# Two transformer blocks on one core: masks by TensorE, table spread by SyncE, token halves at a layer's beginning, rests of weights by GpSimd

## What is computed

```python
h = x @ w_in        # 1024 -> 4 branches' q, k, v, four gates, a merge vector
y_mla = causal softmax attention(low-rank q, k, v with rms norm and rope)
y_sb  = stick-breaking attention: A[t,s] = sigmoid(z[t,s]) * prod_{s<j<t} (1 - sigmoid(z[t,j])), s < t
y_fox = causal softmax attention with log_decay = cumsum(log_sigmoid(f))
y_mem = softmax attention over 256 memory rows
merged = sum_n sigmoid(merge_r @ w_merge_up)_n * ((y_n * silu(gate_n)) @ w_branch[n])
x = layer_norm(alpha * x + merged @ w_out)
```

```python
z = rms_norm(x) @ w_in_2
o_a = softmax attention (rms-normed q, k, axial rope)
o_b = softmax attention in a window of 128 with a sink
o_c = neighbourhood attention with a table of relative position biases (rpb_c)
o_d = (softmax(q1 k1) - lam * softmax(q2 k2)) v, then rms norm
x = x + concat(o_n * silu(g_n)) @ w_out_2       # and a final rms norm at the end
```

## Time and profile before

| | us |
|---|---|
| runs | 1534.04, 1537.66, 1539.85 |
| the profiled execution | 1534.89 |
| its span, first to last instruction | 1533.1 |
| TensorE busy | 1413.1 (92%) |
| VectorE busy | 869.9 (57%) |
| ScalarE busy | 709.6 (46%) |
| GpSimd busy | 366.7 (24%) |
| mean granted TensorE clock | 0.975 of full speed |

### The profile page before, as it was taken

How to read it: one execution, slowest core, us unless ns; L and a number is a source line. 1 busy time by engine, 2 the same in 40 slices (tenths; PEclk the granted TensorE clock), 3 DMA queues, 4 the chain that set the end, 5 groups by cost and what they waited for, 6 DMA issues and landing times.

```text
span 1533.1 us, 21207 instructions
## 1 busy us (share of the span) xinstructions
PE 1413.1 (92%) x8026; PEld 1091.0 (71%) x8026; DVE 869.9 (57%) x1657; ACT 709.6 (46%) x1525; POOL 366.7 (24%) x265
## 2 busy tenths in 40 slices
PE   7999899999989999999997899988998899988997
PEld 6767576777977677777786766665776766665776
DVE  4555337467662553465577565457656465557655
ACT  3555345455234554455543454445444344445443
POOL 2232131245231322223541112320111112320111
PEclk9999999999999999999998899998999899998999
DMA  6413620225242221112263232511313332411311
GB/s 227 111 30 87 158 83 15 78 67 213 97 151 56 52 88 56 55 45 62 91 214 98 60 77 48 111 56 49 97 62 111 83 76 53 99 55 49 97 63 55
DMA packets 191121, 131.73 MB, mean 86 GB/s; under 512 B 91436, under 2 KB 181164, under 8 KB 191020
## 3 DMA queue, kind: packets, MB, share of 16 engines
q1 hardware_dynamic: 179534, 112.29, 26.3%
q10 hardware_dynamic: 11486, 18.09, 3.7%
HBM read 118.03 MB, written 12.32 MB: 85 GB/s over the span
## 4 chain that ended last, share of the span: by engine, by line
PE 69%; DVE 17%; ACT 8%; issue 3%; DMA 1%; ACTq 1%; POOL 0%; DVEq 0%; POOLq 0%
PE pb L1399 18%; PE pb L1400 16%; PE pb L1401 16%; PE pb L1477 6%; PE pb L1421 5%; PE pb L1455 4%; ACT prob L1533 3%; ACT wh L1552 2%; ACT tmp L1533 1%; DVE wl L1897 1%; DVE small L2143 1%; DVE prob L2156 1%; DVE xl L1904 1%; DVE scr L2166 1%; DMA wr<-w_out 1%
## 5 line engine op out<-in xcount | busy, mean ns | idle before, releaser
L2300 POOL TENSOR_TENSOR wl<-wr,wh 128x512 fp32r<-128x512 f32 x170 | 236.4, 1390 | 886.2 <-ACT wh L1552 882.8
L1399 PE MATMUL pb<-xh,wl 128*128 128x512 f32 (+1 forms) x832 | 350.9, 422 | 25.5 <-DVE xl L1904 21.9
L1400 PE MATMUL pb<-xl,wh 128*128 128x512 f32 (+1 forms) x832 | 321.7, 387 | 0.0
L1401 PE MATMUL pb<-xh,wh 128*128 128x512 f32 (+1 forms) x832 | 321.7, 387 | 0.0
L1897 DVE TENSOR_TENSOR wl<-wr,wh 128x512 fp32r<-128x512 f32 x200 | 161.1, 807 | 198.7 <-ACT wh L1552 198.4
L1399 PEld LDWEIGHTS pb<-xh,wl 128*128 128x128 f32 x832 | 162.0, 195 | 103.7 <-issue 50.1
L1552 ACT CAST wh<-wr 128x512 fp32r<-128x512 f32 x370 | 211.1, 603 | 29.3 <-PE pb L1401 23.8
L1401 PEld LDWEIGHTS pb<-xh,wh 128*128 128x128 f32 x832 | 161.7, 194 | 31.7
L1400 PEld LDWEIGHTS pb<-xl,wh 128*128 128x128 f32 x832 | 162.4, 195 | 24.3 <-issue 3.8
L1533 ACT ACTIVATE prob<-prob,small 128x512 f32<-128x512 f32 (+3 forms) x128 | 76.3, 596 | 148.5 <-DVE small L2120 139.1
L1455 PE MATMUL pb<-cst,prob 128*128 128x128 f32 x768 | 120.8, 279 | 22.3 <-ACT prob L1533 8.4
(11 more groups left out here) (196 smaller groups left out, 2446.5 us busy)
## 6 DMA issues: line engine op xcount, KB each, us to landing
wr<-w_in SPq DMA_DIRECT2D x39, 1024.0 KB, 5.1
wr<-w_in SPq DMA_DIRECT2D x48, 256.0 KB, 4.6
wr<-w_out SPq DMA_DIRECT2D x10, 1024.0 KB, 6.4
wr<-w_branch SPq DMA_DIRECT2D x48, 128.0 KB, 2.3
x<-prob SPq DMA_DIRECT2D x12, 512.0 KB, 2.6
wr<-w_out SPq DMA_DIRECT2D x48, 128.0 KB, 2.9
wr<-w_mem_kv SPq DMA_DIRECT2D x4, 1024.0 KB, 5.6
prob<-x ACTq DMA_DIRECT2D x2, 2048.0 KB, 10.2
```

Source lines behind the costliest of these rows:

```text
L1399: e.matmul(ps, ll, rh, start=start, stop=False)
L1400: e.matmul(ps, lh, rl, start=False, stop=False)
L1401: t = e.matmul(ps, lh, rh, start=False, stop=stop)
L2300: t = e.tensor_tensor(wl[:, j % 2, c0:c1], wr[:, j % 2, c0:c1], wh[:, j % 2, c0:c1].bitcast(F32), ALU.subtract)
```

## The change

It has eight parts.

- **Rests of weights.** `by_gpsimd(j, c)` sends all chunks to GpSimd except the even chunks of the first two tiles and of `mr`, `mga` and `mgb`. Whoever waits for rests now waits for each engine's last one (`rests_made`).
- **Masks of the stick-breaking attention.** A matmul of an identity with a 128x128 mask of -1e30 (`strict`) adds the mask to the diagonal block of the logits in PSUM. The maximum in the running product and the multiplication L2169 go. The two constants are copied to `identr` and `strict` by VectorE in the step `lambdas`, which now comes after the projection `sbq`.
- **The spread of the table** is issued by SyncE in eight pieces of 15 rows, two behind each load of weights, from the first layer's MLA stage on.
- **Starts of layers.** For branch A of the second block two weight tiles (`Ag` and `Aq`) are multiplied with tokens 0 to 255 before tiles 2 and 3 of the tokens are transposed. The second layer of the first block now begins in halves too, with tile 3 alone in between.
- **The end of a layer of the second block.** The last column part (m = 3) of `wo2a` for token tiles 2 and 3 is left out of `out_partial` and done after token tiles 0 and 1 are summed (`out_left`).
- **Newton steps** have one operation less, and their first operation no longer waits for the root.
- **MLA's norms.** The copy to `yh` and the rests of it (`normhi`) are put in the list 5000 ns of estimated TensorE time after the normalization.
- **Smaller ones.** `foxrow` goes from VectorE to ScalarE; `dmix` takes the reciprocal and the ratio of both halves in one operation each, after the exps of both; the square for A's norm takes its buffer from another ring.

```diff
-    put("after", np.concatenate([np.zeros((P, 384)), c >= p], 1))
+    put("strict", np.where(c >= p, NEG, 0.0))
...
+    def spread(n):
+        for _ in range(n):
+            if st["spread"] in range(8):
+                put("spread", l=st["spread"] // 4, r=15 * (st["spread"] % 4))
+                st["spread"] += 1
...
+    def halves(w, ep, half, held):
+        for c in range(2):
+            drain(gemm("fm", w, 128 * c, 128 * c + 128, ("x", ep), range(8), n=256, b=held[c], off=256 * half,
+                       end=half == 1))
...
             put("normed", l=l, b=b, tm=tm, tn=tn, dim=dim, grp=grp, gain=gain)
             give(b, tm, tn)
+            ready = now() + 5000
+            for _ in range(40):
+                if now() < ready:
+                    yield
+            put("normhi", l=l, grp=grp)
...
-        if l:
-            held = [drain(gemm("fm", w, 128 * c, 128 * c + 128, ("x", l), range(8))) for c in range(2)]
-        else:
-            held = opened(w, l, lambda: last_features(l, *X))
+        held = opened(w, l, lambda: last_features(l, X, (3,) if l else (2, 3)))
...
-            for turned in ((0, 1), (2,), (3,), ()):
+            for turned in ((0, 1), (2,), ()):
...
-        for x in gate(br + "g", ep, br, l, (lambda: last_features(ep)) if br == "A" else None):
+        two, held = [None, None], [(), ()]
+        if br == "A":
+            two, held = [wnext(br + "g"), wnext(br + "q")], [[GR[0].take() for _ in range(2)] for _ in range(2)]
+            st["hold"] = True
+            for w, h in zip(two, held):
+                halves(w, ep, 0, h)
+            last_features(ep)
+            halves(two[0], ep, 1, held[0])
+        for x in gate(br + "g", ep, br, l, two[0], held[0]):
             if x is not None:
                 box["u"] = x
             yield
+        if br == "A":
+            st["hold"] = False
+            halves(two[1], ep, 1, held[1])
...
+    def out_left(l, w, i):
+        b = drain(gemm("tok", w, 0, 256, ("y2", l), range(6), tile=i))
+        put("acc", l=l, m=3, i=i, b=b)
+        give(b)
...
         for i in range(4):
+            if i == 2:
+                for n in (2, 3):
+                    out_left(l, box["w"], n)
+                    advance_late(late)
+                wdone(box["w"])
+                st["hold"] = False
...
+    def by_gpsimd(j, c):
+        return c % 2 == 1 or not (j < 2 or WEIGHTS[j][0] in ("mr", "mga", "mgb"))
...
+                if br == "sb":
+                    w.wait_ge(v_fn, v_fn.at("masks"))
+                    for b in s["b"]:
+                        t = e.matmul(bank(b)[:, 128 * i:128 * i + 128], identr[:, :], strict[:, :], start=False, stop=True)
                         t.then_inc(logit.sem, logit.mark(b))
...
-                    t = e.tensor_tensor_scan(lo[:, ::-1], x[:, ::-1], m[:, ::-1], 1.0, ALU.mult, ALU.max)
+                    t = e.tensor_tensor_scan(lo[:, ::-1], x[:, ::-1], x[:, ::-1], 1.0, ALU.mult, ALU.bypass)
...
+            elif k == "spread":
+                l, r = s["l"], slice(s["r"], s["r"] + 15)
+                w.wait_ge(d_z, d_z.at("z"))
+                src = zrow[r, l, :].unsqueeze(1).to_broadcast([15, 64, P])
+                e.dma_start(zscr[l][r], src).then_inc(d_spread.sem, d_spread.mark("z"))
```

More of the change, by code:

```diff
@@ L314, in plan @@
     SM = Ring([Slot(i) for i in range(3)])
-    st = {"i": 0, "split": 0, "load": 0, "hold": False}
+    st = {"i": 0, "split": 0, "load": 0, "hold": False, "spread": -1}
     due, aside = [], []
@@ L372, in advance_late @@
         return [g for g in late if next(g, g) is not g]
+    def halves(w, ep, half, held):
+        for c in range(2):
+            drain(gemm("fm", w, 128 * c, 128 * c + 128, ("x", ep), range(8), n=256, b=held[c], off=256 * half,
+                       end=half == 1))
     def opened(w, ep, between):
         held = [GR[0].take() for _ in range(2)]
[L377 to L382, removed]
+        halves(w, ep, 0, held)
+        between()
+        halves(w, ep, 1, held)
         return held
@@ L404, in features, with gate @@
             yield
-    def gate(name, ep, br, l, between=None):
-        w = wnext(name)
-        held, u = opened(w, ep, between) if between else [], None
+    def gate(name, ep, br, l, w=None, held=()):
+        u = None
+        w = wnext(name) if w is None else w
         for c in range(2):
@@ L788, in plan, with last_features @@
         run(features(0, i, (X[i],)))
-    def last_features(ep, *src):
-        for i in (2, 3):
+    def last_features(ep, src=(), tiles=(2, 3)):
+        for i in tiles:
             run(features(ep, i, src and (src[i],)))
@@ L831, in sb_proj @@
             yield from gate_into(box, "g1", "sb", l)
+            yield from proj_fm("sbq", l, "sb", "q", l, False)
             if l == 0:
                 put("lambdas")
-                put("spread")
-            yield from proj_fm("sbq", l, "sb", "q", l, False)
             yield from proj_fm("sbk", l, "sb", "k", l, True)
@@ L967, in project @@
             c0 = 128 * (n % 2)
-            b = yield from beside(gemm("fm", w, c0, c0 + 128, ("x", ep), range(8)))
+            if br == "A" and n < 2:
+                b = held[1][n]
+            else:
+                b = yield from beside(gemm("fm", w, c0, c0 + 128, ("x", ep), range(8)))
             tm = TM.take()
-            sq = TM.take() if br == "A" else None
+            sq = TA.take() if br == "A" else None
             put("pair", l=l, br=br, n=n, b=b, tm=tm, sq=sq)
@@ L2294, in gpsimd_program @@
                 e.memset(zrow[:, :, :], 0.0).then_inc(p_fn.sem, p_fn.mark("zrow"))
-            elif k == "cast" and s["c"] % 2:
+            elif k == "cast" and by_gpsimd(s["j"], s["c"]):
                 j, c = s["j"], s["c"]
```

126 lines of the change are left out of this document (65 added, 61 removed).

## The result

The changed kernel takes 1533.45 us (median of 20 runs), the kernel before beside it 1539.22: a ratio of 0.9967 [0.9955, 0.9978], 5 us less. That is no change by the bound named in the prediction (0.5%), which had said 1506 and 31 us less. The profiled execution took 1530.05 us, its span 1528.2 against 1533.1.

A forecast was written before the change was run, and what follows sets the result against it. TensorE, busy 1413.1 of 1533.1 us, was taken as the bound, leaving 120 us of gaps plus clock losses; -6.5 - 9 - 5 - 7 + 3 - 2 - 3 - 1.5 = -31 gave 1506 us, range 1488 to 1529.

The forecast's parts named there:

- lateness of rests elsewhere: Tiles whose casts come all at once: last GpSimd rest 2.8 us later; +3 us charged, bounds 0 and +40.
- the end: Kernel's end: tiles 0 and 1 done earlier and Newton steps shorter; -1.5 us, bounds 0 to -3.
- Step 2: Second block's start, twice: two tiles' first halves cover the normalization of tokens 256 to 511; -4.5 us each, -9.
- rival A: Layer starts and D: waits only move, behind ScalarE's casts and GpSimd's rests; -15 us in all, 1522; chance 0.22.
- Step 4: 154 rests move from VectorE to GpSimd; 3.5 us of D's idle time out per layer, -7, plus +3 for lateness.
- a mark of failure: Wrong if TensorE's waits for GpSimd's wl exceed 10 us, D's gaps stay at 13, or all gaps exceed 105.
- Step 5: Stick-breaking attention: mask matmuls add +4 us, a lighter VectorE takes -6 of idle; sum -2, bounds +7 to -8.
- Step 3: First block's layer 1 start: mkv1 and mq's first half cover the 4.25 us gap; -5 us, bounds -8 to +2.
- Step 1: 158 to 170 us: spread's DMAs leave ScalarE, TensorE's 5.21 us gap goes; -6.5 us, bounds -8 to +3.
- step 6: MLA's norm: halved waits remove the 2.1 us gap near 110 and its twin; -3 us, bounds -4 to 0.

The follow-up runs named there:

- e11: e7 with wo2a's last two token tiles no longer held back, made where they were before: 0.9832 of the kernel before.
- e7: e4 with VectorE making the even rests again for wo, wo2b, mkv0, mkv1, mq, Aq and Dg: 0.983 of the kernel before.
- e2: The changed kernel with token tiles 2 and 3 transposed between the first halves of Ag and Aq: 0.9921 of the kernel before.
- e1: The changed kernel with A's rope tables loaded at the beginning of its projection, ahead of the weights' casts and loads: 0.9915 of the kernel before.
- e4: The changed kernel with both edits, rope tables loaded early and tiles 2 and 3 transposed between the first halves: 0.9865 of the kernel before.
- e9: The changed kernel with A's starts as before: only Ag in halves, Aq whole, rope tables where they were: 0.9902 of the kernel before.
- the second trace: The changed kernel profiled once more, nothing altered, beside the experiments: 0.9971 of the kernel before, profiled span 1534.5 us.
- e10: The kernel before with only the rests moved to GpSimd (all tiles but 0, 1, mr, mga, mgb): 1.0027 of the kernel before.
- e15: e4 with all rests divided as before, even chunks by VectorE and odd by GpSimd: 0.9814 of the kernel before.
- e13: e7 with all rests of Cg, Cq, Ck and Cv by VectorE, so GpSimd makes none while D runs: 0.9851 of the kernel before.
- e17: e4 with the old division of rests, D's old mixing and layer 1's old start: 0.9834 of the kernel before.
- e18: e17 with the stick-breaking masks on VectorE as before: 0.9814 of the kernel before.
- e8: e4 with the stick-breaking masks back on VectorE: 0.9883 of the kernel before.
- e12: e7 with the first block's layer 1 begun as before, tile 3 behind the memory's parts, mq whole: 0.9805 of the kernel before.
- e16: e7 with layer 1 begun as before and no tiles of wo2a held back: 0.9827 of the kernel before.
- e6: The kernel before with only the table's spread by SyncE, eight pieces, two behind each weight load: 0.9955 of the kernel before.

## Why the prediction was wrong, step by step

By the table's stages, forecast and measured, in us: the spread -6.5, -6.4; the norms -3, -4.0 (-1.8 and -2.2, some of the first being clock); layer 1's start -5, -2.1; the two starts of A -9, **+7.7**; D -7, -5.9; lateness of rests elsewhere +3, +1.8 (A, B, MLA); masks and stick-breaking -2, +1.1; the end -1.5, +3.2. Together -31 and -4.6, against a span 4.9 shorter.

- **Step 2 failed, and is 17 of the 26 us.** Ag's first half starts 10.5 us earlier than before, so 10.5 us are added here to the times of the trace to set them beside the forecast's. Three things in it were wrong.
  First, "VectorE's chain up to there gets shorter" by 4.7 us, so that Aq's casts start near 845.7. They start at 839.58, which is 850.1 in the forecast's time, where 850.38 was before: 0.3 was gained. From tile 0's transposes to Ag's first half the kernel took 15.6 us before and 14.7 after, and the stretch ahead of that was 1.2 us longer. VectorE's own rest is gone from the chain, but the chain now waits for ScalarE behind four casts and runs beside four rests of GpSimd (the one-column operation of 1.20 us takes 0.22 elsewhere, the scaling of 2.18 takes 1.28):
```profile
819.21 2.16 ACT L1612 CAST wh<-wr 128x512 fp32r<-128x512 f32 x4
819.96 5.77 POOL L2353 TENSOR_TENSOR wl<-wr,wh 128x512 fp32r<-128x512 f32 x4 [18.68 <-ACT wh L1612]
822.55 0.15 DVE L1934 TENSOR_SCALAR stats<-stats 128x1 f32<-128x1 f32 x1 [1.19 <-ACT prob L1593]
823.20 1.20 DVE L1937 SCALAR_TENSOR_TENSOR stats<-stats 128x1 f32<-128x1 f32 x1 [0.50 <-ACT stats L1593]
824.63 2.18 DVE L2150 SCALAR_TENSOR_TENSOR setB<-prob,stats,scr 128x1024 f32<-128x1024 f32 x1
```
  In none of the runs' traces does Ag's first half start less than 90.4 us behind the last fox product (91.6 before). At the second start the held tiles of wo2a were to bring it forward by about 4 us: without them (e11) it starts 76.6 us behind C's first product, with them (e7) 76.0.
  Second, the transposes of tiles 2 and 3 were seen to be late ("to about 855"), but began at 861 in the forecast's time: the 4.7 us, and some 1.3 more that the two halves took. The second halves came 5.4 us later than the 859.3 forecast. e2 prices the transposes behind Aq's half at 7 us.
  Third, it didn't follow the rope tables' DMA at all: SyncE's queue was looked at for the spread and not for the tables. e1 prices that at 8 us. With both mended the starts measure -8.0 for the -9 forecast (e4); 1.2 of that is there with A's starts as before (e9). The rival A ("the waits only move") named ScalarE's casts and GpSimd's rests, which are in the first of the three; it had neither of the other two, and -4 as its price.
- **Step 4, rests to GpSimd: the sign was wrong.** -7 + 3 was forecast for D and lateness together. In D the idle time fell by 3.3 us (29.0 to 25.7; in the second trace 25.1), half of the 7. That the stages are 5.9 shorter is in part luck: they had 13.7 us at the low clock for 20.5 before, and in e4, with the same D and 27.3 us at the low clock, they are 0.5 shorter. The move alone makes the kernel before 4 us slower (e10), and undoing it on e4 gives 8 us (3 to 13, e15). Two things that it brought can be seen: 15.4 us of TensorE's waits, which the forecast named as a mark of failure (over 10, as it did gaps of over 105 in all, which are 109.1), and longer VectorE instructions with two inputs in SBUF: the mixing (752 to 1005 ns, together with its new form) and the prefix sum of fox (1216 to 2247 ns before and after, and 1216 again in e15). How the 8 us divide between them is not shown:
```profile
L2026 DVE TENSOR_TENSOR_SCAN fz<-tmp 36x512 f32<-36x512 f32 x2 | 2.4, 1216 | 0.1
```
```profile
L2092 DVE TENSOR_TENSOR_SCAN fz<-tmp 36x512 f32<-36x512 f32 x2 | 4.5, 2247 | 0.1
```
  The first rest of a tile that is needed at once is the dear one: a GpSimd rest takes 1.36 us in the mean, six matmuls of 256 columns 0.7. The Trainium skill ("SBUF — State Buffer", "Who interferes with whom") says that such a VectorE instruction and one of GpSimd that reads SBUF block each other; the forecast quoted it, wrote that by it the old division would be the better one, and then set 0 to 10 us at next to nothing. The traces bear the rule out in the durations. What e13 adds is that in D the blocking alone costs little time. D's lighter VectorE does end 3 us of idle time (25.5 in e4 for 28.7 and 27.9 in e15 and e17), but whether that is time gained can't be told: the stages take 184 us for 182 and 183, with 27.3 us at the low clock for 13.7 and 20.5.
- **Step 5, masks.** Two mask matmuls take 0.28 us in the trace, 4.5 for all 32, as costed (+4). The -6 for waits was too much: idle time fell by 1.4 us as changed, since moving the rests at the same time takes some of it back (5.2 us idle in e15, 7.6 in e4), by 2.6 where the rests stay divided (e18 to e17), and by 3.7 where they are GpSimd's on both sides (e8 to e4). All three are less than 4.5.
- **Step 3** measured 2.1 in its stage; the runs of e12 and e16 can't tell it from nothing. The gap of 4.25 us became one of 1.56, but the stage's idle time fell by 1.0 only (7.5 to 6.5): TensorE's waits for GpSimd's rests in it went from 0.2 to 4.4 us.
- **The end.** wo2b's rests come from GpSimd and TensorE waits for them at each layer's end:
```profile
1156.98 0.47 PE L1454 MATMUL pb<-wh,yl 128*128 128x512 f32 x1 [0.55 <-POOL wl L2353]
...
1159.68 0.47 PE L1454 MATMUL pb<-wh,yl 128*128 128x512 f32 x1 [1.77 <-POOL wl L2353]
```
  In e7, which gives them back to VectorE, 0.7 us of the 2.3 are left. This tile was named nowhere in the forecast: it is used as soon as it is opened.
- **Step 1 and the norms of step 6 were right** in place and about in size: step 1 by e6, the norms by the gap near 110 and its twin, which are gone; no run takes them alone.

What stays open: 16 us between as changed and e4 by the runs is 9.8 us by idle time. Part of the rest may be the clock behind each gap, but single traces of one kernel differ by as much as 20.8 us in time at the low clock, so this is argued and not shown.

## What to carry to other kernels

When a step is taken forward, list every instruction that it drags along, and for each queue ask what now stands behind it that had nothing to wait for: here two table loads of 256 KB behind a weight load cost more than the whole change brought. A chain that crosses engines is not shortened by the sum of what leaves one of them: 4.7 us of VectorE's work were to bring Ag's start forward, and brought it nothing, since ScalarE's casts and GpSimd's rests stood in the same chain. A tile that must be ready at once wants its parts from two engines, whatever the average load of either says. And measure the parts one by one: the whole change gave 5 us, one part of it alone 7, and the same change with two steps moved in its order 21.

## What the runs showed of the hardware

TensorE's idle time in one kernel repeats to 0.2 us between two traces (by stage, to 0.6) while its span differs by 6.3; what differs with it is where and how long the granted clock is at its low level (1.2 GHz and not 2.4), 56.1 and 76.9 us. For parts of a few us, idle time by stage tells more than a span, or than a median with an interval of 0.2%.
A half of a tile costs little over the whole: matmuls of 256 columns follow each other at 0.119 us in e4's trace, those of 512 at 0.228, so a pair of halves costs 0.01 us more.
